# Two transformer blocks on one core: first norm in token layout, x transposed twice, first-branch buffers re-homed, tiles placed alike modulo 256

## The reference, cut to what matters

```python
h = rmsnorm(x, norm_mix)                      # mean of squares over the 1024 features of a token
zu, zv, zq, zf, zi, zo, g_a, g_b = split(h @ w_in)
y_a = gmlp_branch(zu, zv, ...) @ w_up_a       # GELU(u) * (W_s LayerNorm(GELU(v)) + b)
y_b = hgrn2_branch(zq, zf, zi, zo, ...) @ w_up_b   # 8 heads, chunkwise linear recurrence
x = x + (sigmoid(g_a) * y_a + sigmoid(g_b) * y_b) @ w_out
x = x + square(relu(rmsnorm(x, norm_ffn) @ w_ff1)) @ w_ff2
x = rmsnorm(x, final_norm)
# second block: an mLSTM layer of 4 heads, an RG-LRU layer of 4 groups, a last rmsnorm
```

## Time and profile before

| | us |
|---|---|
| median of three runs | 1816.34 (1815.55 to 1820.97) |
| the profiled execution's own time | 1819.99 |
| its span, first to last instruction | 1818.3 |
| PE busy | 1706.8 (94%) |
| DVE, ACT, POOL busy | 859.6, 824.7, 860.1 |

### The profile page before, as it was taken

One profiled execution on the slowest core, in us unless ns is written; L12 is line 12 of the kernel. 1 busy time (PEld: TensorE's weight loads), 2 busy tenths in 40 slices (PEclk: granted clock), 3 DMA queues, 4 the chain that ended last, 5 costly groups with the idle time before them and its releaser, 6 DMA issues.

```text
span 1818.3 us, 21831 instructions
## 1 busy us (share of the span) xinstructions
PE 1706.8 (94%) x7685; PEld 1373.9 (76%) x7685; DVE 859.6 (47%) x1324; ACT 824.7 (45%) x1084; POOL 860.1 (47%) x1094
## 2 busy tenths in 40 slices
PE   3968999999999999999999999999999979989977
PEld 2756888887888888888887777877877757777865
DVE  4244766761112321211145658267167276656853
ACT  3334777773234432322246645345345335654562
POOL 4413233334665654555565636436446435356740
PEclk9988999998999999999999999999999989999998
DMA  5202112111333333333333322322322314033211
GB/s 153 75 19 81 58 58 69 52 53 58 93 100 105 96 93 93 98 99 93 92 92 93 81 59 72 102 61 91 93 63 89 93 32 110 23 107 95 70 35 47
DMA packets 251094, 142.93 MB, mean 79 GB/s; under 512 B 6161, under 2 KB 249618, under 8 KB 251026
## 3 DMA queue, kind: packets, MB, share of 16 engines
q1 hardware_dynamic: 251026, 142.00, 27.0%
HBM read 139.89 MB, written 2.10 MB: 78 GB/s over the span
## 4 chain that ended last, share of the span: by engine, by line
PE 81%; DVE 8%; ACT 6%; issue 4%; POOL 1%; ACTq 0%; DVEq 0%; POOLq 0%
PE bank L733 23%; PE bank L735 23%; PE bank L734 23%; PE bank L1044 2%; PE bank L830 2%; ACT w_hi L1138 2%; DVE ee L1762 1%; DVE qk L1776 1%; PE bank L1023 1%; PE bank L1085 1%; PE bank L1008 1%; PE bank L1006 1%; PE bank L1007 1%; DVE qk L1777 1%; PE bank L1086 1%
## 5 line engine op out<-in xcount | busy, mean ns | idle before, releaser
L717 POOL TENSOR_TENSOR w_lo<-raw,w_hi 128x256 fp32r<-128x256 f32 x1056 | 846.1, 835 | 911.8 <-ACT w_hi L1138 911.5
L1138 ACT ACTIVATE w_hi<-raw 128x1024 fp32r<-128x1024 f32 x264 | 277.5, 1056 | 614.3 <-PE bank L735 578.4
L733 PE MATMUL bank<-h_hi,w_hi 128*128 128x512 f32 x1304 | 525.3, 403 | 26.8 <-POOL w_lo L717 14.3
L735 PE MATMUL bank<-h_hi,w_lo 128*128 128x512 f32 x1304 | 512.7, 393 | 0.0
L734 PE MATMUL bank<-h_lo,w_hi 128*128 128x512 f32 x1304 | 512.6, 393 | 0.0
L733 PEld LDWEIGHTS bank<-h_hi,w_hi 128*128 128x128 f32 x1304 | 247.8, 190 | 90.7 <-issue 28.4
L734 PEld LDWEIGHTS bank<-h_lo,w_hi 128*128 128x128 f32 x1304 | 248.1, 190 | 54.9 <-issue 4.3
L735 PEld LDWEIGHTS bank<-h_hi,w_lo 128*128 128x128 f32 x1304 | 247.4, 190 | 52.7
L1864 DVE TENSOR_TENSOR xT<-xT,bank 128x512 f32<-128x512 f32 x104 | 68.5, 684 | 239.4 <-PE bank L735 239.1
L733 PE MATMUL bank<-f_hi,w_hi 128*128 128x512 f32 x256 | 101.3, 396 | 0.0
L734 PE MATMUL bank<-f_lo,w_hi 128*128 128x512 f32 x256 | 101.3, 396 | 0.0
(11 more groups left out here) (349 smaller groups left out, 2607.1 us busy)
## 6 DMA issues: line engine op xcount, KB each, us to landing
raw<-in_w_ff SPq DMA_DIRECT2D x64, 512.0 KB, 4.0
raw<-in_w_in SPq DMA_DIRECT2D x56, 512.0 KB, 3.8
raw<-in_m_w_in SPq DMA_DIRECT2D x48, 512.0 KB, 4.0
raw<-in_r_w_in SPq DMA_DIRECT2D x24, 512.0 KB, 3.8
raw<-in_m_w_out SPq DMA_DIRECT2D x16, 512.0 KB, 3.5
raw<-in_r_w_out SPq DMA_DIRECT2D x16, 384.0 KB, 3.2
raw<-in_w_up_b SPq DMA_DIRECT2D x8, 512.0 KB, 4.2
raw<-in_w_out SPq DMA_DIRECT2D x8, 512.0 KB, 4.2
```

Of the source, the lines that this page charges most:

```text
L717: ins = pool.tensor_tensor(w_lo[:, s, part], raw[:, s, part], w_hi[:, s, part].bitcast(F32), ALU.subtract)
L733: pe.matmul(dst, wh, hi[:, k, :], start=(k == 0), stop=False)
L735: mm = pe.matmul(dst, wl, hi[:, k, :], start=False, stop=(k == kt - 1))
L1138: act.activation(w_hi[:, p % RING, :], raw[:, p % RING, :], ACT.Copy).then_inc(hi_ready[p % RING], 1)
```

## The change

1. The first norm is taken where x arrives. ACT squares `xtok` (128x1024, four tiles) with a row sum as second output, takes Ln and Exp of the four columns, and scales one tile into `xn`; DVE scales the other three. PE turns x into `xT` as before (now first of all, as soon as `ident` and x are there) and turns the scaled `xn` as well (32 more transposes). ACT forms `h_hi` and DVE `h_lo` straight from PSUM, with the gain as scale. The products with `ones`, `hf` and `norm_upper`/`norm_apply` of this norm are gone. The last four turned tiles are issued inside the first `dense`.
2. POOL no longer clears `raw`; it makes `ident` first. SP issues panel 0 right behind x, then the gains' sheet, panels 1 to 3, the other two sheets, `ws` and the rest. The turns of sheets 1 and 2 and of `ws` come after panel 1 on PE; the byte masks on DVE after the norm.
3. An Ln with no use of its own stands first on ACT, before x is there.
4. Ln and Exp of the LayerNorm variance come after the second `gu`, not after the fourth.
5. `upper(11)` comes before the `ya_hi` copies; ACT no longer waits for all of `ya` before `head_soft(0)`; `upper(12)` and `upper(13)` come before `head_decays(0)`, `upper(14)` before `head_z(0)`. For this `wsT`, `yg`, `bn`, `xtok`, `sheets`, `maskf` are put at other places of the stage area.
6. Tile sizes are rounded to 64 bytes, small tiles are moved behind `hf`, and the stage areas and what follows `xm` and `xr` are put at `raw`'s own remainder modulo 256.

```diff
-        place = [(nc.sbuf_base + 63) // 64 * 64]
+        place = [(nc.sbuf_base + ROW // 2 - 1) // ROW * ROW + ROW // 2]
-            size = (size * (1 if dt == U8 else 4) + 31) // 32 * 32
+            size = (size * (1 if dt == U8 else 4) + 63) // 64 * 64
...
+        assert (base - raw_at) % ROW == 0
...
         xm = sb("xm", [P, MT, PAD + S], F32, a)
+        a[0] = base + (a[0] - base + ROW - 1) // ROW * ROW
...
         xr = sb("xr", [P, RT, PAD + S], F32, a)
+        a[0] = base + (a[0] - base + ROW - 1) // ROW * ROW
...
-            sp.wait_ge(raw_zero, 1)
-            for j in range(GG):
+            load(G_P, w_in[:, 512:512 + P], 8, P)
+            rows((0,), gains_loaded)
+            for j in range(1, GG):
                 load(G_P + j, w_in[:, 512 + j * P:512 + (j + 1) * P], 8, P)
+            rows((1, 2), rows_loaded)
...
-            pool.memset(raw[:], 0.0).then_inc(raw_zero, 1)
+            steps.link(pool.memset(ident[:], 0.0))
+            pool.affine_select(out=ident[:], in_=ident[:], ...).then_inc(ident_made, 1)
...
+            def turn_normed(j):
+                if j < 4:
+                    aux_released(pe, 4 + j, 3 if j == 0 else 2)
+                else:
+                    pe.wait_ge(h_made, j - 3)
+                for n in range(NT):
+                    mm = pe.transpose(bank[4 + j % 4][:, n * P:(n + 1) * P], xn[:, n, j * P:(j + 1) * P], ident[:])
+                mm.then_inc(xn_turned, 1)
+            def turn_ahead(k):
+                if k + 4 < DT:
+                    turn_normed(k + 4)
+                pe.wait_ge(h_made, k + 1)
...
+            turn_sheet(0)
+            pe.wait_ge(xn_act, XN_ACT)
+            pe.wait_ge(xn_dve, NT - XN_ACT)
+            for j in range(4):
+                turn_normed(j)
+            dense(G_P, G_T, need=turn_ahead)
+            dense(G_P + 1, G_T + 1)
...
+            act.activation(small[:, 1:2], eps, ACT.Ln)
+            act.wait_ge(x_loaded, 16 * NT)
+            for n in range(NT):
+                act.activation(xn[:, n, :], xtok[:, n, :], ACT.Square,
+                               accum_out=small[:, 2 + n:3 + n]).then_inc(ss_made, 1)
             upper(0)
+            act.wait_ge(ss_made, NT)
+            link(act.activation(small[:, 2:2 + NT], small[:, 2:2 + NT], ACT.Ln, bias=eps, scale=1.0 / D))
+            act.activation(small[:, 2:2 + NT], small[:, 2:2 + NT], ACT.Exp, scale=-0.5).then_inc(rstd_made, 1)
+            act.wait_ge(rstd_made, 1)
+            for n in range(XN_ACT):
+                act.activation(xn[:, n, :], xtok[:, n, :], ACT.Identity, scale=small[:, 2 + n:3 + n])\
+                   .then_inc(xn_act, 1)
             upper(1)
+            for j in range(DT):
+                act.wait_ge(xn_turned, j + 1)
+                act.wait_ge(gain_made, 1)
+                act.activation(h_hi[:, j, :], bank[4 + j % 4][:], ACT.Identity, scale=col("norm_mix", j))\
+                   .then_inc(hi_made, 1)
             upper(2)
...
+                if j == 1:
+                    act.wait_ge(var_made, 1)
+                    link(act.activation(lnv, bn[:, :, 7], ACT.Ln, bias=eps))
+                    act.activation(lnv, lnv, ACT.Exp, scale=-0.5).then_inc(rs_made, 1)
+            upper(H_P + 3)
...
-            act.wait_ge(ya_made, GG)
             head_soft(0)
-            upper(H_P + 3)
+            upper(H_P + 4)
+            upper(H_P + 5)
             head_decays(0)
             head_v(0)
-            upper(H_P + 4)
-            upper(H_P + 5)
+            upper(H_P + 6)
             head_z(0)
-            upper(H_P + 6)
...
+            for n in range(XN_ACT, NT):
+                dve.tensor_scalar(xn[:, n, :], xtok[:, n, :], small[:, 2 + n:3 + n], None, ALU.mult).then_inc(xn_dve, 1)
+            for j in range(DT):
+                dve.wait_ge(hi_made, j + 1)
+                dve.scalar_tensor_tensor(h_lo[:, j, :], bank[4 + j % 4][:], col("norm_mix", j),
+                                         h_hi[:, j, :].bitcast(F32), ALU.mult, ALU.subtract).then_inc(h_made, 1)
```

## The result

The changed kernel takes 1766.49 us (median of 4 executions, 1765.29 to 1767.70); the kernel before took 1817.14 us beside it (1815.55 to 1820.97). The ratio is 0.971, 95% interval 0.9698 to 0.9721: faster by 2.9%. The time lies in the range, 13.5 us above the 1753 that I called likeliest.

What follows compares the result with a forecast made beforehand. PE bounds the kernel from 600 to 1000 us, waits bound the start. 23.6 - 0.9 + 10.5 + 17.0 + 13.5 = 63.7 us off 1820.0 gives 1756.3 profiled, median 1753; 8 in 10 from 1742 to 1770.

Steps and rivals of the forecast that it cites:

- places give nothing: Rival: 396 against 389 ns belongs to the stage, so the new operand places gain nothing; time 1766, chance 0.12.
- Part 1: Start up to panel 1: the new norm chain starts panel 1 at 31.2 us instead of 54.85, 23.6 us gained.
- lock: Rival at the start: DVE's scalings wait for POOL's w_lo pieces, xn at 22.4, 2.7 us less gained; chance 0.12.
- Part 2: Between panels 1 and 2: turning sheets 1 and 2 and ws moves onto PE's path, 0.9 us lost.
- Part 3: Variance two panels earlier: vn starts sooner and heads begin at 101.5 instead of 113.04, 10.5 us gained.
- My bound for a slow `vn`: Before the heads: vn slowed beside POOL by up to 0.3 us an operation; with low clock only 6.2 us gained.
- Part 4: Head 0: reordered ACT work has panels ready without waits, transposes 35.1 us after the heads begin, 17.0 us gained.
- the 35 us that I had named as the sign of error: Head 0: the prediction is wrong if head_v(0) comes later than 35 us after the first head product.
- the clock takes part of it back: Rival: new PE pauses before xn, at vn and head 0 lower the clock, costing 8 to 15 us; chance 0.10.
- Part 5: Split matmuls of seven tiles: zero distance between operands takes 396 ns to 389, 13.5 us gained.
- The term for `xm`: 384 half-length matmuls on xm: 1.2 us gained if each gains half as much as a full-length one.
- The slower rival: Rival: engines collide at one shared remainder and every split matmul pays; 1877 us at twice the break-even price, chance 0.02.

Runs made afterwards that it cites:

- the places undone: Changed kernel with the stage areas again 224 bytes from raw's remainder modulo 256, and what follows xm and xr at 32: 1778.14 us, ratio 0.9774.
- vT too: Changed kernel with head_v(0) ahead of head_decays(0) and, for head 0 alone, head_vT(0) right behind the decays: 1764.20 us, ratio 0.9686.

## Why the prediction was right, and where it was not

The time is in the range and the five parts are real, but the closeness owes something to luck. My 1753 missed by 13.5 us, and 1766 is also what I gave for the rival "places give nothing". By the time alone that rival would have won; the 389 ns and the places undone exclude it.

- **Part 1 was right**: 24.1 us for 23.6. `xn` came at 18.86 us, not 19.7. The rival that the chances call "lock", with the cast of the earlier trace rows as the model for the scalings, happened in a small way and cost 0.5 us, not 2.7: only the third scaling was slowed beside POOL, and it took 1.22 us for 0.75. The scaling, which started 0.12 us into a POOL piece, took 0.46 us longer, and the POOL piece behind it 0.45 us longer: less than one piece (0.72), not the four of a panel. Why the cast took as long as twelve pieces and the scaling did not, no row shows.
- **Part 2 was right**, 0.8 for 0.9 us.
- **Part 3 came short by 1.4 us** at its own place, 9.1 for 10.5, for two reasons. `vn` took 11.6 us, where I took 10.8 (64.63 to 76.23): seven of its eight operations on two SBUF tiles took 1.06 to 1.11 us beside POOL where the eighth took 0.69. That is 0.4 us each for the 0.3 that I had as the high end. (My bound for a slow `vn` charged 0.3 to all twelve operations, 12.4 us; the eight that I named give 11.2.) And the last 26 mixing products took 4.4 us (76.28 to 80.64) at a granted clock of 0.65, where I counted 2.8 and held 1.0 back for the clock.
- **Part 4 is the step that failed, and in it the clock.** Up to the transposes it gave 15.4 of 17.0 us; `vf` came 36.4 us after the first head product, not 34.4, past the 35 us that I had named as the sign of error. What I priced at nothing was the pause that I saw coming ("2.4 at head 0" stood only in the rival): behind it the transposes, the two parts of the levels and panel 14 took 0.5 + 0.8 + 5.6 + 2.5 = 9.4 us longer than at full clock. Net, part 4 is worth 6.0 us by the table and 7.1 by undoing it. My rival "the clock takes part of it back" gave 1761 to 1768 and the time is 1766.5: that rival happened, with one long drop in the place of three, and I gave it 0.10.
- **What the experiments show of the cause.** The twice longer products are the clock: with the same order and the same pause the 56 products take 12.05 us where the granted clock is 0.50 and 7.20 where it comes back to 1.00 after some 3 us, and in neither profile does PE wait for VectorE or for a bank among them. Without a pause before them (vT too) they take 6.36. The price of the pause was not fixed: the stretch from panel 13 to 15 is 13.0 us longer than without a pause in the changed kernel's profile and 5.1 to 5.3 us in the two executions with a short low stretch. A prediction could have given the range, but no run shows what would let it choose.
- **The parts do not add up one by one.** Undoing part 3 alone costs 1.3 us by the medians though it brings 9.1 at its place, because that version's low stretch was short.
- **Part 5 was right as a mechanism**: 13.9 us by the panel starts, 11.6 by undoing it, for 13.5. All seven tiles went from 396 to 389 ns. The term for `xm` had the wrong sign: its products take 283 ns now, 281 before and with the places undone.
- "From the second head on" I had PE ending last. That was only nearly true. With the pauses of head 0 gone, PE waited 3.13 us for `so`, then 2.76 for the square and 0.86 for bank 7, all within a head.
- The slower rival, engines colliding at one remainder, is excluded by the 389 ns.

## What to carry to other kernels

Price a pause of TensorE by what stands behind it at the lower clock, not by its length, and as a range: here about 3.4 us of waiting cost between 2 and 9 us more, in executions that differ in nothing else at that place. Do not judge such a place by one profile. When a wait is taken away, follow the engine that was late down its list to the next thing it makes, and the next: here it took three moves (`vf`, `vT`, `so`), with `xm` moved as well, until the time was clearly below that of the changed kernel. And compare instructions per window at equal clock between two placements of the operands: the windows tell distances 64 and 128 apart (1334 and 1320) where the durations do not (394 ns both).

## What the runs showed of the hardware that I had not expected

- The step of a split matmul depends on how far apart the stationary and the moving operand begin modulo 256 bytes. For 512 columns it is 226.7 ns from start to start at 0, 229.0 at 64, and 233.3 at 128 and at 224 (durations 389, 394, 394 and 396 ns). For 256 columns the median durations are 283 at 0, 282 at 128, 281 at 32, and 276 or 281 in two runs at 64. Why, no run shows.
- The same pause, 3.42 to 3.46 us, was followed by 56 products in 12.05 us in four profiled executions and in 7.20 and 6.53 us in two others; one of those two has the same order of work as the four. A pause of 3.13 us was followed by no fall at all (1.00 in the 17 us behind it), and waits of 1.18 and 1.01 us by a low stretch (0.67 in the 4.1 us behind the first, 0.83 in the 10 us around the second). The clock's stay at the lower level is not read from the length of the pause.
- What POOL beside DVE costs depends on the form of DVE's operation and on how they meet, and mostly both pay. With two SBUF inputs, 128x256 goes from 0.42 to 0.96 us and 128x512 from 0.69 to 1.1, while POOL's pieces go from 0.72 to as much as 1.19. The 128x512 `TENSOR_SCALAR` that reads a bank for `vn` took 0.81 us without POOL and 0.80 beside it. A 128x1024 `TENSOR_SCALAR` that began inside a piece took 1.22 for 0.75 us. The cast of the earlier trace rows took 8.32 us beside all twelve pieces, which themselves lost nothing: 8.21 us for twelve, 0.68 each.
